# Two layers written out, norms by token tile and half row, turned rows in eight banks, last products by tile

## The chip, the core and the metric

The program runs on one core of one Trainium2 chip. The metric is the device time of one execution, in microseconds (us), as the median of several runs. Engines: TensorE (PE), VectorE (DVE), ScalarE (ACT), GpSimd (POOL) and SyncE (SP), which here issues nearly all DMAs. Each runs its own instruction queue in order, and they wait for one another by semaphores.

## The reference

Two models stand one behind the other. The first is a block of two layers over 256 tokens of width 1024; each layer has a mixer of four branches and a convolved FFN, and each of these ends in an RMS norm whose result is added to x.

```python
for l in range(DEPTH):                     # DEPTH = 2
    h = rms_norm(x, norm_mix_pre[l])
    proj = h @ w_in[l]
    ...
    mix = jnp.concatenate([y_conf, y_sb, y_ret, y_sc], axis=-1) @ w_out[l]
    x = x + rms_norm(mix, norm_mix_post[l])
    f = conv_ffn(rms_norm(x, norm_ffn_pre[l]), ffn_up[l], ffn_conv_w[l], ffn_down[l])
    x = x + rms_norm(f, norm_ffn_post[l])
```

The second block takes that x with a second sequence ctx of 256 tokens and conditioning rows (silu(c) @ ada_w): recurrent memory and attention branches, then a mixture of 32 experts. All is float32.

## The kernel before, in words

Tokens lie on the partitions in two tiles of 128 (t = 0, 1), so x is 128 x 2 x 1024. For a projection x is normalised into xhat, TensorE transposes xhat into PSUM, and ScalarE writes the rows times the gain as a rounded "high" part (high_rows, line 912), VectorE what the rounding lost as a "low" part (low_rows, 1246). Weights are split in the same way in units of 128x1024: ScalarE line 923 the high part, VectorE line 1268 the low part, three units in buffers; each product is made in three passes (high x high, high x low, low x high), so an "up" unit is 24 products of 256 columns.

The two layers are one loop on every engine (loop_layers, lines 760 to 762): the instructions stand once, and waits are on values computed from the loop's register. In a layer, TensorE runs transposes "T" (banks 0 to 3), 24 units of w_in, the branches, the mixer's output M (banks 4 to 7, bank i for token tile i // 2 and column half i % 2; tokens_down, slots 6 and 7), transposes "F" (banks 0 to 3), and 66 units of the FFN, of which 22 "down" units add into D (banks 4 to 7).

The norm after the mixer and the FFN: rms_of_banks squares a tile of 1024 columns out of two banks (line 884, then the root, 885), add_normed takes the reciprocal (1207), multiplies both halves out of PSUM by root and gain (1232) and adds to x (1222). After the mixer rms_of_x then squares the new x per tile, normalise_tile scales it (1213), and transposed turns both tiles (1889); the rows go through high_rows and low_rows in eight pieces of 128x256, and TensorE starts the first unit once all eight are done. After the FFN the same stands at the head of the next pass of the loop. keep_clock is a filler: products of a constant 128x384 (line 1869, psum<-const) whose result nobody reads.

The semaphores x_tile_ready and x_ready count the sums for tile 0 and 1. SyncE loads weights in half slots of 1 MB into a ring of five places; a place is free when its units are split, or, for the mixer's output, after tokens_down (slot_free). GpSimd loads the second block's small tensors, ctx and two rows of ada_b (lines 841 to 850). In the second block, ScalarE works in this order: SiLU of c (1015), squares of x, squares of ctx, evacuation of the "ada" rows (904); TensorE makes ada(0), ada(1), then waits for those rows before each further step, turns x and ctx, and starts products (701 us). The experts' weights (line 824 on) are loaded when slots come free.

Of the kernel before, what the change touches and what calls it, by code (L numbers as in the profile page):

```python
# [13 lines left out]
P = 128  # L14
# [20 lines left out]
ACT_STEPS = 9  # L35
DVE_STEPS = 128
# [96 lines left out]
LAYER_BANKS = [("T", i, i) for i in range(4)]  # L133
# [8 lines left out]
LAYER_BANKS += [("F", i, i) for i in range(4)]  # L142
# [171 lines left out]
def build_program(nc, w, out):  # L314

    with ExitStack() as ctx:
# [222 lines left out]
        x_ready = sem("x_ready")  # L539
# [220 lines left out]
        def loop_layers(eng, layer):  # L760
            with eng.Fori(0, DEPTH) as l:
                layer(l)

        @block.sync
        def _(sp):
# [25 lines left out]
            for l in range(DEPTH):  # L791
                for n in range(len(LAYER_SLOTS)):
# [7 lines left out]
                    if n == 13 and l + 1 < DEPTH:  # L800

                        sp.wait_ge(x_ready, 2 * l + 2)
                        load_mixer_columns(sp, l + 1)
                        load_mixer_rows(sp, l + 1)
                    if n == RING and l:

                        sp.wait_ge(x_ready, 2 * l + 1)
# [27 lines left out]
        def _(pool):  # L835
# [5 lines left out]
            pool.wait_ge(x_ready, 2 * DEPTH)  # L841
# [26 lines left out]
        def _(act):  # L868
            n_step = [0]

            def step(ins, l):
# [3 lines left out]
                act.wait_ge(act_step, l * ACT_STEPS + n_step[0])  # L875
# [12 lines left out]
            def rms_of_x(l, n):  # L888

                rms_of([x[:, t, :] for t in range(TT)], l, lambda t: act.wait_ge(x_ready if t else x_tile_ready, n))  # L890
# [6 lines left out]
            def rms_of_banks(l, key):  # L897

                load_root_table()
                rms_of([psum[:, 4 + 2 * t:6 + 2 * t, :].rearrange("p b n -> p (b n)") for t in range(TT)], l,  # L900
                       lambda t: [take(act, (key, 2 * t + i), l) for i in (0, 1)])
# [4 lines left out]
            def high_rows(key, l, n, col):  # L906

                for i in range(4):
                    b = take(act, (key, i), l)
                    for c in (0, 1):  # L910
                        k = 2 * i + c
                        ins = nc.scalar.activation(hT_split[:, 0, k, :], b[:, c * T:(c + 1) * T], ACT.Copy,
                                                   scale=cols[:, col + k:col + k + 1])
                    ins.then_inc(hT_high_ready, 1)

            def layer(l):
                n_step[0] = 0
                def split(n):
                    if n >= UNIT_BUFFERS:
                        after_unit(act, n - UNIT_BUFFERS, l)  # L920
                    raw, h = unit_weights(n, None)
# [3 lines left out]
                split_until = units_ahead(split, UNITS)  # L925
                rms_of_x(l, 2 * l + 1)
                split_until(UNIT_BUFFERS - 1)
# [23 lines left out]
                act.wait_ge(act_step, l * ACT_STEPS + n_step[0])  # L951
# [26 lines left out]
                split_until(MIX_UNITS + UNIT_BUFFERS - 1)  # L978
# [1645 lines left out]
```

## Time and profile before

| what | us |
|---|---|
| median of 3 runs | 2182.85 |
| lowest and highest | 2179.92, 2186.36 |
| the profiled execution | 2183.95 |
| its span, first to last instruction | 2182.2 |
| TensorE busy in it | 2061.6 |
| VectorE busy | 867.3 |
| ScalarE busy | 595.2 |
| mean granted clock of TensorE | 0.981 of full |

The first block takes the first 665 us, the second block without its experts some 570, and the rest is the experts, in which the DMA engines are nearly always busy. Busy times are averages over stages with different limits: what a norm costs is read from the timeline around it, as the time from TensorE's last product to its next. Filler products count as busy.

### The profile page before, as it was taken

The numbers are of one execution on the slowest core, as the hardware profiler recorded it, in microseconds if no ns is written. First come the engines' busy times: TensorE is split into PE (matmuls) and PEld (weight loads), VectorE is DVE, ScalarE is ACT, GpSimd is POOL, SyncE is SP. The second block draws the span as 40 slices with busy tenths as digits, with TensorE's granted clock in tenths as the row PEclk, the third lists the DMA queues.
The fourth block names the chain that finished last, engine by engine and source line by source line (L and its number), as shares of the span: only waits on it lengthen the run. The fifth ranks groups of instructions, "written<-read, shape, count | busy, mean of one in ns | idle before, by whom it ended". The sixth has DMA issues, their size and how long they took to land.

```text
span 2182.2 us, 27676 instructions
## 1 busy us (share of the span) xinstructions
PE 2061.6 (94%) x11094; PEld 1323.7 (61%) x11094; DVE 867.3 (40%) x1510; ACT 595.2 (27%) x962; POOL 11.6 (1%) x23
## 2 busy tenths in 40 slices
PE   8999999999998998899989999999999999999998
PEld 7869998959995776677789533333333333333332
DVE  6847676947675226553622311111111111111111
ACT  4545555445555323342431100000000000000001
POOL 0000000010000000000000000000000000000000
PEclk9999999999998999999999999999999999999999
DMA  7335553355546534021234699999999999999996
GB/s 293 114 135 200 182 174 141 140 171 192 185 163 231 240 148 162 30 78 52 84 116 154 261 413 413 432 432 432 432 431 431 429 431 432 432 432 432 432 432 291
DMA packets 43237, 589.71 MB, mean 270 GB/s; under 512 B 5185, under 2 KB 5873, under 8 KB 9825
## 3 DMA queue, kind: packets, MB, share of 16 engines
q1 hardware_dynamic: 41392, 583.09, 65.5%
q0 software_dynamic: 1456, 5.01, 0.8%
q8 instruction: 67, 1.10, 0.2%
q10 hardware_dynamic: 288, 0.24, 0.0%
q14 instruction: 34, 0.27, 0.0%
HBM read 587.27 MB, written 1.05 MB: 270 GB/s over the span
## 4 chain that ended last, share of the span: by engine, by line
PE 78%; DMA 13%; DVE 4%; issue 2%; ACT 2%; DVEq 0%; SPq 0%; ACTq 0%
PE psum L1869 46%; PE psum L2299 22%; DMA slots<-exp_w_dram 12%; PE psum L2244 3%; PE psum L2336 3%; PE psum L2411 3%; DVE split_weights L1443 1%; DMA slots<-w_in_dram 0%; DMA slots<-ffn_up_dram 0%; DVE work L1569 0%; PE psum L1889 0%; PE psum L2177 0%; DVE work L1586 0%; DVE split_rows L1246 0%; ACT work L1079 0%
## 5 line engine op out<-in xcount | busy, mean ns | idle before, releaser
L2299 PE MATMUL psum<-slots,work 128*64 128x512 f32 x3072 | 687.2, 601 | 47.8 <-DMA slots<-exp_w_dram 46.3
L2299 PEld LDWEIGHTS psum<-slots,work 128*64 128x64 f32 x3072 | 219.9, 138 | 479.8 <-issue 467.1
L1869 PE MATMUL psum<-split_rows,split_weights 128*128 128x256 f32 (+1 forms) x3744 | 489.8, 293 | 13.0 <-DVE split_rows L1495 4.1
L1869 PEld LDWEIGHTS psum<-split_rows,split_weights 128*128 128x128 f32 x3744 | 473.0, 193 | 33.3 <-issue 12.3
L1268 DVE TENSOR_TENSOR split_weights<-slots,split_weights 128x1024 fp32r<-128x1024 f32 x180 | 219.6, 1224 | 161.3 <-ACT split_weights L923 160.6
L923 ACT ACTIVATE split_weights<-slots 128x1024 fp32r<-128x1024 f32 x180 | 189.9, 1058 | 216.7 <-PE psum L1869 179.1
L1869 PE MATMUL psum<-split_weights,split_rows 128*128 128x512 f32 x1008 | 232.3, 390 | 1.0 <-DVE split_weights L1443 1.0
L1869 PEld LDWEIGHTS psum<-split_weights,split_rows 128*128 128x128 f32 x1008 | 188.3, 188 | 42.5 <-issue 2.5
L1831 DVE TENSOR_SCALAR work<-psum 128x512 f32<-128x512 f32 x32 | 22.0, 689 | 401.4 <-PE psum L2299 401.4
L1869 PE MATMUL psum<-work 128*128 128x128 f32 (+9 forms) x964 | 152.7, 335 | 19.9 <-DVE work L1605 7.1
L1869 PEld LDWEIGHTS psum<-work 128*128 128x128 f32 (+2 forms) x964 | 124.3, 196 | 50.4 <-issue 36.9
L1169 ACT ACTIVATE work<-work 128x512 f32<-128x512 f32 x32 | 20.2, 631 | 478.1 <-DVE work L1831 478.1
L1162 ACT ACTIVATE work<-psum,small 128x128 f32<-128x128 f32 x64 | 24.1, 457 | 352.3 <-PE psum L1869 352.3
L1443 DVE TENSOR_TENSOR split_weights<-slots,split_weights 128x1024 fp32r<-128x1024 f32 x64 | 76.5, 1222 | 106.2 <-ACT split_weights L1020 106.0
L904 ACT ACTIVATE work<-psum 128x512 f32<-128x512 f32 (+3 forms) x150 | 76.1, 523 | 156.2 <-PE psum L1869 119.8
L1020 ACT ACTIVATE split_weights<-slots 128x1024 fp32r<-128x1024 f32 x64 | 66.8, 1055 | 108.6 <-DMA slots<-w_in_dram 62.5
L1844 DVE TENSOR_TENSOR work<-psum,work 128x512 f32<-128x512 f32 x32 | 22.2, 692 | 167.3 <-PE psum L2299 167.3
L1869 PE MATMUL psum<-slots,work 128*128 128x512 f32 x192 | 83.6, 593 | 0.0
L1869 PE MATMUL psum<-const 128*128 128x384 f32 (+2 forms) x208 | 73.0, 496 | 11.2 <-DVEq L1861 6.8
L1412 DVE SCALAR_TENSOR_TENSOR work<-psum,work 128x254 f32<-128x254 f32 (+1 forms) x176 | 76.6, 477 | 1.6
L1869 PEld LDWEIGHTS psum<-const 128*128 128x128 f32 (+1 forms) x208 | 39.9, 199 | 39.5 <-issue 14.3
L2244 PE MATMUL psum<-work 128*128 128x512 f32 (+1 forms) x136 | 63.0, 605 | 0.0
(249 smaller groups left out, 1333.3 us busy)
## 6 DMA issues: line engine op xcount, KB each, us to landing
slots<-exp_w_dram SPq DMA_DIRECT2D x95, 4096.0 KB, 19.0
slots<-w_in_dram SPq DMA_DIRECT2D x56, 1024.0 KB, 6.1
slots<-ffn_up_dram SPq DMA_DIRECT2D x44, 1024.0 KB, 4.8
slots<-ada_w_dram SPq DMA_DIRECT2D x24, 1024.0 KB, 7.0
slots<-ffn_down_dram SPq DMA_DIRECT2D x20, 1024.0 KB, 4.9
slots<-w_out_dram SPq DMA_DIRECT2D x12, 1024.0 KB, 5.0
slots<-w_branch_a_dram SPq DMA_DIRECT2D x4, 1024.0 KB, 8.1
slots<-w_branch_b_dram SPq DMA_DIRECT2D x4, 1024.0 KB, 5.0
```

Of the source, the lines that this page charges most:

```text
L904: nc.scalar.activation(out_, in_, func, **kw).then_inc(evacuated[bank_of(key)], 1)
L923: nc.scalar.activation(unit_weights(n, 0), raw, ACT.Copy).then_inc(w_high_ready, 1)
L1020: nc.scalar.activation(unit_weights2(n, 0), unit_weights2(n, None), ACT.Copy).then_inc(w_high_ready, 1)
L1162: ins = nc.scalar.activation(xgT[:, k, :], b[:, k * P:(k + 1) * P], ACT.Identity, scale=scale2[:, k:k + 1], bias=modT[:, 2 * KC + k, 0:1])
L1268: nc.vector.tensor_tensor(unit_weights(n, 1), unit_weights(n, None)[0], unit_weights(n, 0), ALU.subtract).then_inc(w_split, 1)
L1412: ins = nc.vector.scalar_tensor_tensor(out=o, in0=b[:, c * T:(c + 1) * T - k], scalar=cols[:, at:at + 1], in1=o, op0=ALU.mult, op1=ALU.add)
L1443: nc.vector.tensor_tensor(unit_weights2(n, 1), unit_weights2(n, None), unit_weights2(n, 0), ALU.subtract).then_inc(w_split, 1)
L1869: return nc.tensor.matmul(out_, lhsT, rhs, start=first, stop=last)
L2244: return nc.tensor.matmul(psum[:, i, :], lhsT, rhs, start=first, stop=True, skip_group_check=True)
L2299: return nc.tensor.matmul(b[rows, :], lhs[:, rows], rhs, start=first, stop=last, skip_group_check=True)
L2336: nc.tensor.matmul(psum[:, bank_of((key, n)), :], pick_e, b1_rows[:, c0:c0 + 512], start=False, stop=False, skip_group_check=True)
L2411: ins = nc.tensor.matmul(b[:, c * T:(c + 1) * T], hT_split[:, v, 4 * j + k, c * P:(c + 1) * P], wu[a][:, k, :], start=j + c + k + q == 0, ...
```

## The change

1. The loop is gone: each_layer writes the two layers out, and waits are on constants.
2. After mixer and FFN each norm works on half rows of 512: ScalarE squares a bank (half_square), VectorE multiplies it by the gain at once (times_gain) and, when the root is there, multiplies by its reciprocal and adds to x in one instruction (add_to_x). The squares of the new x are taken by halves too. The FFN's end makes the next norm's squares and xhat itself, for the second block too; the second block no longer does.
3. xhat is turned into eight banks, one for each pair of columns and token tile (turn). high_rows and low_rows work in 16 pieces of 128x128 in the order TILE_ORDER, and the first unit waits pair by pair.
4. The mixer's last products run by token tile; the last two down units are multiplied bank by bank.
5. Fillers move: none before the transposes of tile 0 after the mixer, five behind them; five before "T" of the second layer once bank 4 is added; none at the start behind the transposes and none ahead of the second block.
6. Only two units instead of three are split ahead of the mixer's norm, and one of the next layer's ahead of the FFN's norm.
7. Waits on x_ready become waits on evacuations: the loads of mixer parameters on ("M", 3), of FFN parameters on ("D", 3) of the layer before, GpSimd's loads on ("D", 3) of the last layer.

```diff
+TILE_ORDER = ((0, 0), (1, 0), (0, 1), (1, 1), (2, 0), (2, 1), (3, 0), (3, 1))
...
-LAYER_BANKS = [("T", i, i) for i in range(4)]
+LAYER_BANKS = [("T", i, i) for i in range(8)]
...
-        def loop_layers(eng, layer):
-            with eng.Fori(0, DEPTH) as l:
+        def each_layer(layer):
+            for l in range(DEPTH):
                 layer(l)
...
-            pool.wait_ge(x_ready, 2 * DEPTH)
+            after_evacuation(pool, ("D", 3), DEPTH - 1)
...
+            def half_square(rows, t, half, l):
+                i = 2 * t + half
+                n_squared[0] += 1
+                nc.scalar.activation(flat(soft)[:, 0:512], rows, ACT.Square, accum_out=half_sumsq[:, i:i + 1]
+                                     ).then_inc(half_squared, 1)
+                act.wait_ge(half_squared, n_squared[0])
+                if half == 0:
+                    nc.scalar.activation(half_mean[:, t:t + 1], half_sumsq[:, i:i + 1], ACT.Identity, bias=EPS, scale=1.0 / D)
...
-                split_until(MIX_UNITS + UNIT_BUFFERS - 1)
-                rms_of_banks(l, "M")
-                rms_of_x(l, 2 * l + 2)
+                split_until(MIX_UNITS + 1)
+                load_root_table()
+                for t in range(TT):
+                    for square in (square_of_bank, square_of_sum):
+                        square("M", l, t, 0)
+                        square("M", l, t, 1)
+                        root(t)
...
-                rms_of_banks(l, "D")
+                if l + 1 < DEPTH:
+                    splits[l + 1](0)
+                load_root_table()
+                square_of_bank("D", l, 0, 0)
+                square_of_bank("D", l, 0, 1)
+                root(0)
+                square_of_bank("D", l, 1, 0)
+                square_of_sum("D", l, 0, 0)
+                square_of_bank("D", l, 1, 1)
+                root(1)
+                square_of_sum("D", l, 0, 1)
+                root(0)
+                square_of_sum("D", l, 1, 0)
+                square_of_sum("D", l, 1, 1)
+                root(1)
...
+            def add_to_x(l, n, key, t):
+                inverse_rms(n, t)
+                for half in (0, 1):
+                    cut = slice(512 * half, 512 * half + 512)
+                    nc.vector.scalar_tensor_tensor(out=x[:, t, cut], in0=xhat[:, t, cut], scalar=rinv[:, t:t + 1],
+                                                   in1=x[:, t, cut], op0=ALU.mult, op1=ALU.add
+                                                   ).then_inc(evacuated[bank_of((key, 2 * t + half))], 1)
...
-                tokens_down("M", l, 6, catT, (0, 1), False, False, slot_free)
-                after_evacuation(pe, ("RT", 0), l)
-                tokens_down("M", l, 7, catT, (4, 5), False, True, None)
-
-                keep_clock(("F", 0), l, 6)
-                pe.wait_ge(x_tile_ready, 2 * l + 2)
-                keep_clock(("F", 0), l, 3)
-                transposed("F", l, 2, idle=(("D", 0), 5))
+                for t in range(TT):
+                    tokens_down("M", l, 6, catT, (0, 1), False, False, slot_free if t else None, (2 * t, 2 * t + 1))
+                    after_evacuation(pe, ("RT", 0), l)
+                    tokens_down("M", l, 7, catT, (4, 5), False, True, None, (2 * t, 2 * t + 1))
+
+                pe.wait_ge(xhat_tile_ready, 2 * l + 2)
+                turn("F", l, 0)
+                keep_clock(("F", 4), l, 5)
+                pe.wait_ge(xhat_ready, 2 * l + 2)
+                turn("F", l, 1)
```

TensorE's queue from the mixer's last products to the first up unit, before; const rows of 128x384 are fillers:

```order
L1869 MATMUL psum<-slots,work 128x512 [waits half_slot0_loaded,half_slot4_loaded,bank3_evacuated]
L1869 MATMUL psum<-slots,work 128x512 x7
...
L1869 MATMUL psum<-const 128x384 [waits bank0_evacuated]
L1869 MATMUL psum<-const 128x384 x5
...
L1869 MATMUL psum<-const 128x384 [waits bank0_evacuated,x_tile_ready]
...
L1889 MATMUL psum<-const,work 128x128 [waits bank0_evacuated,xhat_tile_ready]
...
L1889 MATMUL psum<-const,work 128x128 [waits xhat_ready]
...
L1869 MATMUL psum<-const 128x384 [waits bank4_evacuated]
...
L1869 MATMUL psum<-split_rows,split_weights 128x256 [waits bank0_evacuated,weights_split]
```

The same place in the changed kernel, from the transposes on:

```order
L1944 MATMUL psum<-const,work 128x128 [waits bank0_evacuated,xhat_tile_ready]
...
L1911 MATMUL psum<-const 128x384 [waits bank4_evacuated]
L1911 MATMUL psum<-const 128x384 x4
L1944 MATMUL psum<-const,work 128x128 [waits bank4_evacuated,xhat_ready]
...
L1911 MATMUL psum<-split_rows,split_weights 128x256 [waits bank0_evacuated,bank4_evacuated,weights_split]
L1911 MATMUL psum<-split_rows,split_weights 128x256 x5
L1911 MATMUL psum<-split_rows,split_weights 128x256 [waits bank5_evacuated,bank1_evacuated]
...
L1911 MATMUL psum<-split_rows,split_weights 128x256 [waits bank6_evacuated,bank2_evacuated]
...
L1911 MATMUL psum<-split_rows,split_weights 128x256 [waits bank7_evacuated,bank3_evacuated]
```

The fillers ahead of tile 0's transposes are gone, five stand between the tiles, and the first unit's products wait in four steps.

GpSimd's queue ahead of the second block, before:

```order
L847 DMA work<-gate_w_dram 128x128 [waits x_ready]
L847 DMA work<-const_dram 128x1120
...
L847 DMA work<-router_b_dram 128x32
L848 DMA work<-ctx_dram 128x2x1024
L850 DMA work<-ada_b_dram 128x1024 x2
```

And changed:

```order
L846 DMA work<-gate_w_dram 128x128 [waits bank7_evacuated]
L846 DMA work<-const_dram 128x1120
...
L846 DMA work<-router_b_dram 128x32
L847 DMA work<-ctx_dram 128x2x1024
L849 DMA work<-ada_b_dram 128x1024 x2
```

The order is the same; the first wait moved from the second mixer's sum (x_ready 4) to bank 7 of the last FFN.

## Rows read from the trace of the kernel before

**Rows 1.** Page part 4: the chain that ended last, by engine.

```profile
PE 78%; DMA 13%; DVE 4%; issue 2%; ACT 2%; DVEq 0%; SPq 0%; ACTq 0%
```

**Rows 2.** Timeline, first mixer end: start us, us, engine, line, operation, [idle before, releaser].

```profile
116.95 13.90 PE L1869 MATMUL psum<-slots,work 128*128 128x512 f32 x32
...
128.95 1.06 ACT L923 ACTIVATE split_weights<-slots 128x1024 fp32r<-128x1024 f32 x1 [9.31 <-DMA slots<-ffn_up_dram]
...
131.43 1.01 ACT L884 ACTIVATE work<-psum 128x1024 f32<-128x1024 f32 x1
...
133.00 1.41 DVE L1232 SCALAR_TENSOR_TENSOR work<-psum,stats,work 128x512 f32<-128x512 f32 x2
...
141.64 3.03 ACT L912 ACTIVATE split_rows<-psum,work 128x256 fp32r<-128x256 f32 x8 [1.77 <-PE psum L1889]
...
142.58 3.23 DVE L1246 SCALAR_TENSOR_TENSOR split_rows<-psum,work,split_rows 128x256 fp32r<-128x256 f32 x8 [1.73 <-ACT split_rows L912]
...
146.45 18.80 PE L1869 MATMUL psum<-split_rows,split_weights 128*128 128x256 f32 x153
```

**Rows 3.** Timeline, first FFN end and the loop's jump.

```profile
333.40 5.97 PE L1869 MATMUL psum<-const 128*128 128x384 f32 x18
...
337.66 1.28 ACT L884 ACT_TABLE_LOAD   x1 [2.65 <-issue]
...
350.71 7.45 PE L1869 MATMUL psum<-split_rows,split_weights 128*128 128x256 f32 x60 [0.70 <-issue]
```

**Rows 4.** Timeline, from the last FFN to the second block.

```profile
665.00 4.03 PE L1869 MATMUL psum<-const 128*128 128x384 f32 x12
...
673.49 1.06 ACT L884 ACTIVATE work<-work 128x1024 f32<-128x1024 f32 x1 [1.15 <-DVE work L1213]
...
676.05 1.07 ACT L904 ACTIVATE work<-psum 128x512 f32<-128x512 f32 x2
...
701.36 13.02 PE L1869 MATMUL psum<-split_rows,split_weights 128*128 128x256 f32 x96 [4.07 <-DVE split_rows L1495]
```

**Rows 5.** Timeline, the kernel's last norm: squares of half rows on ScalarE.

```profile
2174.04 0.58 ACT L1179 ACTIVATE work<-psum 128x512 f32<-128x512 f32 x1
...
2174.85 0.58 ACT L1179 ACTIVATE work<-psum 128x512 f32<-128x512 f32 x1
...
2175.55 0.29 ACT L1182 ACTIVATE stats<-stats 128x1 f32<-128x1 f32 x1
```

**Rows 6.** Groups by line: 128x128 pieces; busy and mean ns, then idle.

```profile
L1162 ACT ACTIVATE work<-psum,small 128x128 f32<-128x128 f32 x64 | 24.1, 457 | 352.3 <-PE psum L1869 352.3
...
L1698 DVE SCALAR_TENSOR_TENSOR work<-work,small 128x128 f32<-128x128 f32 x16 | 4.3, 352 | 0.0
```

**Rows 7.** Timeline, the start of the first layer.

```profile
10.77 2.18 PE L1889 MATMUL psum<-const,work 128*128 128x128 f32 x16
...
15.02 3.22 DVE L1246 SCALAR_TENSOR_TENSOR split_rows<-psum,work,split_rows 128x256 fp32r<-128x256 f32 x8
...
18.43 11.77 PE L1869 MATMUL psum<-split_rows,split_weights 128*128 128x256 f32 x96 [1.61 <-DVE split_rows L1246]
```

**Rows 8.** Stretches: busy us (instructions) of each engine, then PEclk, DMA share, GB/s.

```profile
342.00:344.00 2.00, 1.34 (x7) 1.34 (x7) 1.64 (x4) 1.97 (x5) 0.00 (x0) 0.60 0.00 0
...
702.00:704.00 2.00, 2.00 (x11) 2.00 (x11) 1.60 (x3) 0.33 (x2) 0.00 (x0) 0.50 0.00 0
```

**Rows 9.** Timeline of GpSimd: its loads for the second block.

```profile
471.05 0.68 POOL L847 DMA_DIRECT2D work<-gate_w_dram  x1 [469.87 <-DVE x_row L1222]
...
474.86 0.71 POOL L848 DMA_DIRECT2D work<-ctx_dram  x1
```

**Rows 10.** DMA issues: xcount, KB each, median us to landing; then GpSimd's loads.

```profile
work<-ctx_dram POOLq DMA_DIRECT2D x1, 1024.0 KB, 9.6
...
small<-cT_dram SPq DMA_DIRECT2D x1, 8.0 KB, 19.4
...
DMA to landing us min/median/max: 2.2/4.6/10.8
```

More of the change, by code:

```diff
@@ L141 @@
 LAYER_BANKS += [("CM", 0, 1), ("CV", 0, 2), ("RT", 0, 3)]
-LAYER_BANKS += [("F", i, i) for i in range(4)]
+LAYER_BANKS += [("F", i, i) for i in range(8)]
 LAYER_BANKS += [("U", g, (2 * (g // 2)) % 4 + g % 2) for g in range(6)]
@@ L886, in rms_of, with rms_of_x @@
                                          ).then_inc(rms_ready, 1)
-            def rms_of_x(l, n):
-                rms_of([x[:, t, :] for t in range(TT)], l, lambda t: act.wait_ge(x_ready if t else x_tile_ready, n))
+            def rms_of_x(l, loaded):
+                rms_of([x[:, t, :] for t in range(TT)], l, loaded)
             def load_root_table():
@@ L923, in split, with layer @@
                     nc.scalar.activation(unit_weights(n, 0), raw, ACT.Copy).then_inc(w_high_ready, 1)
-                split_until = units_ahead(split, UNITS)
-                rms_of_x(l, 2 * l + 1)
-                split_until(UNIT_BUFFERS - 1)
+                return units_ahead(split, UNITS)
+            splits = [layer_splits(l) for l in range(DEPTH)]
+            def layer(l):
+                split_until = splits[l]
+                if l == 0:
+                    act.wait_ge(x_loaded, 16)
+                    rms_of_x(l, lambda t: None)
+                    split_until(UNIT_BUFFERS - 1)
                 act.wait_ge(mix_cols_loaded, 16 * l + 16)
@@ L1269, in split, with layer @@
                                             ).then_inc(w_split, 1)
-                split_until = units_ahead(split, UNITS)
-                normalise(l, 0, 2 * l + 1)
-                split_until(UNIT_BUFFERS - 1)
+                return units_ahead(split, UNITS)
+            splits = [layer_splits(l) for l in range(DEPTH)]
+            def layer(l):
+                split_until = splits[l]
+                if l == 0:
+                    for t in range(TT):
+                        normalise_tile(t + 1, t)
+                    split_until(UNIT_BUFFERS - 1)
                 dve.wait_ge(mix_cols_loaded, 16 * l + 16)
@@ L1860, in _ @@
             dve.wait_ge(x_loaded, 16)
-            dve.sem_inc(x_tile_ready, 1)
-            dve.sem_inc(x_ready, 1)
-            loop_layers(dve, layer)
+            each_layer(layer)
             second()
@@ L1878, in keep_clock, with transposed @@
                     mm(b[:, 0:SPARE], ident, const[:, 0:SPARE])
-            def transposed(key0, l, n, rows=xhat, wait=True, idle=None):
+            def transposed(key0, l, n, rows=xhat, wait=True):
                 for t in range(TT):
@@ L1914, in diagonal_scores, with tokens_down @@
                     done(mm(bs[m][:, T:DIAG], keysT[rows[m], c, P:T], queries[rows[m], c, P:T]), (key, 2 * c + m))
-            def tokens_down(key, l, n, lhs, ks, first, last, free):
+            def tokens_down(key, l, n, lhs, ks, first, last, free, banks=range(4)):
                 wt = slot_ready(pe, n, l, 4)
-                for i in range(4):
+                for i in banks:
                     t, half = divmod(i, 2)
@@ L2528, in _ @@
             pe.wait_ge(zeros_ready, 3)
-            loop_layers(pe, layer)
+            each_layer(layer)
             second()
```

187 lines of the change are left out of this document (102 added, 85 removed).

## Prediction

> **What bounds the kernel now.** First the chain that ended last by line [rows 1]: 78% of it is TensorE, and 22 + 12 points of it are the experts (line 2299 and the DMA of their weights), which the change doesn't touch. Those loads go out when slots come free, so what the part before them wins or loses moves the end by the same amount. I therefore look for the places in the first 700 us at which TensorE has no product to make. There are five, each a norm: the start, the end of mixer and FFN in two layers, and the hand-over to the second block.
>
> At the end of the first mixer [rows 2] the last product's row is 116.95 + 13.90 = 130.85, and the next product starts at 146.45: 15.6 us. Between them stand in a row: squares on ScalarE, which start only at 131.43 because ScalarE first splits a third unit whose half slot is late (128.95, "9.31 idle <-DMA"); sixteen transposes; eight high parts 141.64 to 144.67; eight low parts 142.58 to 145.81. At the first FFN's end [rows 3] it is 333.40 to 350.71, 17.3 us, and ScalarE loads a table at 337.66 after 2.65 us "issue", which is the loop's jump. The loop's second pass has the same rows at its mixer end. At the hand-over [rows 4] products of rows start 701.36 - 665.00 = 36.4 us after the last FFN product.
>
> **The change, part by part.** All times below are on the clock of this trace; its span is 2182.2, its execution 2183.95, and the median of the runs 2182.85, so 1.1 less.
>
> *Mixer end.* The last products now run by tile, so banks M0 and M1 are whole after 6 and 8 of 16 products. One product is 13.90/16 = 0.87: M0 at 122.2, M1 at 123.9, M2 at 129.1, M3 at 130.85. ScalarE splits two units instead of three and is free by 121.2. A half's square with its mean is 0.81 from issue to issue, and its root starts 0.70 after the square [rows 5]. Two multiply-adds of 512 take 1.41 on VectorE [rows 2], and I take half of it, 0.70, for the new multiply of 512 as well; 0.2 for a reciprocal, 0.8 for a normalised tile. Tile 0: squares 122.35 and 124.05, root 124.75, multiply-adds 125.7 to 127.1, squares of the sum, root 128.0, normalised 129.3, all under tile 1's products; transposes follow the last product at 131.0. Five keep-clock products of 0.67 hold TensorE until 135.4. Tile 1: squares 129.25 and 131.0, root 131.7, multiply-adds 132.6 to 134.0, squares of the sum 133.4 and 134.2, root 134.9, normalised 136.25, transposed from 136.35. Now the turned rows, by tile in 16 pieces of 128x128 on each engine. VectorE's is 0.26 (sixteen of line 1698 in 4.3, less 0.35 for the last, by 15) [rows 6]. For ScalarE no row has this form: the 256-column piece is (3.03 less some 0.48 for the last one's own length)/7 = 0.364 [rows 2], the row of a 512 square (0.58) lies 0.43 under that of a 1024 square (1.01 [rows 2]), so 128 columns less are 0.11 less, 0.26; line 1162, 128x128 but with one more operand, comes in fours: 24.1/16 = 1.506, less 0.457, by 3 = 0.35 [rows 6]. I take 0.26, from the row that differs in size alone, and keep 0.35 as the upper bound. Piece (0, tile 1) can start at 136.8; six tiles of two pieces end at 139.9, VectorE at 140.5, and the last 6 of the unit's 24 products (0.123 each) end at 141.3. Before, that unit ended at 146.45 + 2.95 = 149.4. **Gain 8.1**, with 0.35 instead of 0.26 7.0. The third unit's split follows the high parts (139.9 to 142.2) and is wanted at 144.2: hidden. Its load waits for slot_free, now 3.5 us later (127.4), and lands near 132: hidden too.
>
> The ScalarE page of the Trainium skill ("ScalarE: Activation LUTs", What ACT_TABLE_LOAD costs) prices such a piece at 186 + 107 + 93 - 93 = 293 ns, by which the gain would be some 0.3 smaller; no run here shows that form.
>
> *First FFN end.* The last two units are multiplied by bank: 24 products in 5.5 us make D0 at 329.2, D1 330.6, D2 332.0, D3 333.35. ScalarE first splits the next layer's unit 0 (328.0 to 329.1), then table, squares 330.4 and 331.2, root 331.9; VectorE adds tile 0 at 332.8 to 334.2 and tile 1 at 336.0 to 337.35; roots of the sum at 336.05 and 338.2; normalised 338.2 and 339.55; transposes 338.3 and 339.65. High parts end at 343.2, low 343.85, unit 0 at 344.65; unit 1, whose split now stands behind the high parts, runs 345.6 to 348.5. Before, unit 1 ended at 350.71 + 5.9 = 356.6. **Gain 8.0.** The loop's jump and two table loads go with it. The convolution taps wait on constants now, but line 1297 already runs at VectorE's pace, so the unrolling brings nothing there.
>
> *Start.* Low parts from 15.02 [rows 7]: the first pair of tiles at 16.6, all at 19.2, unit 0 ends at 20.0 instead of 21.4: 1.4. But TensorE's six keep-clock products of 4 us are gone, and it idles from 12.95.
>
> *The clock.* After the keep-clock products end at 339.4 [rows 3] TensorE idles, and in 342 to 344 the granted clock is 0.60, partly 1.2 GHz [rows 8]; it comes back before the products. At the hand-over the products after 701.36 themselves run at 0.50, 1.2 GHz. In the changed kernel the fillers before the mixer's transposes are gone and products start into whatever clock is left. A slow stretch costs 0 to 1.7 us (the slow stretch around 703 held some 3.4 us, of which half is lost). I charge 0.8 at each layer's norm and 1.1 at the start: start +0.3, mixers 2 x 7.3, FFN 7.2. Sum of gains 22.1.
>
> *Hand-over.* Here the change takes time. GpSimd's loads for the second block waited for the second mixer (x_ready 4: issued from 471.05 [rows 9], 200 us before use). They now wait for bank D3's evacuation in the last layer. By the steps above that is 668.5. Queued behind this wait are six small loads, 3.81 us of issue, then the 1 MB of ctx, then the two rows of ada_b. ctx lands 9.6 us after issue [rows 10]: 668.65 + 3.81 + 9.6 = 682.1. ScalarE squares it (before at 673.49), and behind those squares on ScalarE stand the evacuations of the ada rows (676.05 [rows 4]), for which TensorE waits before the next ada product. 2.56 us as before plus 1.28 for a table that the SiLU, now after the roots, evicts: 685.9 instead of 676.05, 9.9 late. SyncE's ada loads, which before found no other queue, share the engines then; ctx by equal sharing lands some 2 us later still. **Loss 12.** Below: the median landing of GpSimd's loads, 4.6, would make it 4.9 for ctx. Above: an 8 KB load issued in the full queue of the start landed after 19.4 [rows 10], which would make it 19.7.
>
> The DMA page of the Trainium skill ("DMA: Bandwidth & Descriptors", Anatomy of one DMA - SWDGE (gpsimd) path) fits 2.0 us + bytes/436e3 for such a load, 4.4 for ctx. By it the loss would be near 5, which is the first rival below; the row's 9.6 has other transfers in flight, and here there are more.
>
> **Sum:** 2183.95 - 22.1 + 12 = 2173.9, so 2174.
>
> **The rivals.**
> *The late loads cost little.* For it: most of the small loads land sooner than ctx, and TensorE idles here anyway while ScalarE works off the norms. Against it: in the trace ctx took 9.6 us without SyncE's loads beside it. With a loss of 5: 2183.95 - 22.1 + 5 = 2166.9.
> *The gain per norm is half.* The clock is low at every boundary and 128-column pieces take 0.35: 8.1 - 1.1 - 1.7 = 5.3 each, 15.9 with the start at -0.5 15.4; loss 14: 2182.5, no measurable change.
> *The late loads cost more than all norms give, the slower case.* One mechanism: the software queue's loads, ctx and ada_b, share with SyncE's 1 MB halves, and VectorE waits for both ada_b rows before it scales ctx. With gains of 22.1 the kernel is slower from a landing of 9.6 + 12.2 = 21.8 us on, and measurably from 28; the 19.4 of the start is near. With 30 us: 2192.
> *The change doesn't do what it says:* half rows bring no overlap because banks still come whole at the end. The order of products speaks against it: M0 is whole 8.6 us before M3. Included in the second case.
>
> **How the numbers follow.** About 0.3% (6.5 us) is what a measurement can tell from no change. Forecast 0.60 (its own range 2169 to 2178.5), little loss 0.13, half gain 0.22, slower 0.05. Net gains over 6.5 us are the first two and a little of the third: faster 0.74, same 0.21, slower 0.05. The range leaves out the far ends: the best sum, 25.7 - 8 = 17.7, is 2166, and the half-gain case 2182.5: 2166.5 to 2182.5.
>
> **What would show it.** In the changed trace: the gap from the last mixer product to the end of the first up unit near 10.5 us instead of 18.5, twice; from the last FFN product of layer 0 to the end of the second unit near 15 instead of 23; GpSimd's first load near 647 (668.65 less the 22 won before it) instead of at a mixer's end, behind VectorE's add; ctx's squares waiting for a DMA; 128x128 ScalarE pieces at 0.25 to 0.35. It is wrong if GpSimd's loads start at the mixer's end, if ctx's squares don't wait for them, or if the granted clock stands at half for more than 3 us at a norm.

## The result

| | before | changed |
|---|---|---|
| median of 4 runs, us | 2183.07 | 2165.62 |
| lowest and highest | 2179.92, 2186.36 | 2163.21, 2167.73 |
| the profiled execution's span | 2182.2 | 2164.5 |

The changed kernel is 17.45 us faster, ratio 0.992, 95% interval 0.9901 to 0.9938 (13.5 to 21.6 us). Timed once more in five rounds it was 2165.37 against 2179.89: ratio 0.9929, 0.9914 to 0.9944 (12.2 to 18.7 us). The forecast was 2174.0, 9 us under the median and 10 under the profiled execution, and the range ended at 2166.5: the direction was right and the size too small, by 8.4 us.

**The profile after.** Page part 4, the chain by engine, answers to [rows 1]:

```profile
PE 79%; DMA 13%; DVE 5%; ACT 2%; issue 1%; POOL 0%; SPq 0%; DVEq 0%; ACTq 0%
```

Timeline of the changed kernel, first mixer end (start us, us, engine, line, operation, [idle before, releaser]), against [rows 2]:

```profile
117.54 13.90 PE L1911 MATMUL psum<-slots,work 128*128 128x512 f32 x32
...
122.89 0.60 ACT L900 ACTIVATE work<-psum 128x512 f32<-128x512 f32 x1 [1.15 <-PE psum L1911]
...
129.04 0.75 DVE L1251 TENSOR_SCALAR work<-x_row,stats 128x1024 f32<-128x1024 f32 x1
129.76 0.60 ACT L900 ACTIVATE work<-psum 128x512 f32<-128x512 f32 x1 [0.95 <-PE psum L1911]
...
135.91 0.75 DVE L1251 TENSOR_SCALAR work<-x_row,stats 128x1024 f32<-128x1024 f32 x1
...
137.19 3.21 ACT L929 ACTIVATE split_rows<-psum,work 128x128 fp32r<-128x128 f32 x12 [0.49 <-PE psum L1944]
...
138.61 7.62 PE L1911 MATMUL psum<-split_rows,split_weights 128*128 128x256 f32 x58 [0.80 <-DVE split_rows L1279]
```

The mixer's products end at 131.44. Tile 0's first square starts at 122.89, 8.6 us ahead of that, and its rows are normalised by 129.8. The first product of the FFN starts 7.2 us after the mixer's last one; before it was 15.6.

The first FFN's end, against [rows 3]:

```profile
326.14 3.49 PE L1911 MATMUL psum<-const 128*128 128x384 f32 x10 [0.20 <-DVE x_row L1267]
330.81 1.09 PE L1944 MATMUL psum<-const,work 128*128 128x128 f32 x8 [1.18 <-DVE work L1251]
332.20 1.09 PE L1944 MATMUL psum<-const,work 128*128 128x128 f32 x8 [0.30 <-DVE work L1251]
334.09 3.53 PE L1911 MATMUL psum<-split_rows,split_weights 128*128 128x256 f32 x24 [0.80 <-DVE split_rows L1279]
338.15 4.10 PE L1911 MATMUL psum<-split_rows,split_weights 128*128 128x256 f32 x32 [0.52 <-DVE split_weights L1300]
```

The hand-over, against [rows 4] and [rows 9]:

```profile
645.89 0.68 POOL L846 DMA_DIRECT2D work<-gate_w_dram  x1 [644.71 <-DVE x_row L1267]
...
648.45 6.17 PE L1911 MATMUL psum<-slots,small 128*32 128x512 f32 x32 [6.26 <-ACT small L1055]
...
652.15 2.87 SPq L787 DMA_DIRECT2D slots<-ada_w_dram  x3
...
658.79 1.06 ACT L883 ACTIVATE work<-work 128x1024 f32<-128x1024 f32 x1 [10.40 <-DMA work<-ctx_dram]
...
662.64 1.07 ACT L921 ACTIVATE work<-psum 128x512 f32<-128x512 f32 x2
663.32 1.84 PE L1911 MATMUL psum<-work 128*128 128x2 f32 x8 [8.70 <-issue]
```

GpSimd's loads start at 645.89, ctx's squares wait 10.40 us for a DMA, and the evacuation of the ada rows (662.64) stands behind them. The first product that uses such a row starts at 663.32, 21.1 us after the first block's end. The second block's first product from split rows starts at 688.15.

**Where the time went**, by stage, from TensorE's timelines of five executions. "The third slot's end" is the end of the products made from the first three weight slots of a layer; "hand-over" is the time from the last FFN product to the second block's first product from split rows. Stage ends are modelled ends of products, so they can differ by 0.2 from a row's.

| stage, us | before | before again | changed | again | again |
|---|---|---|---|---|---|
| start to the third slot's end | 41.6 | 41.9 | 42.2 | 42.3 | 41.2 |
| last mixer product to first down product, layer 0 | 50.4 | 50.3 | 42.2 | 42.2 | 42.2 |
| last down product to the third slot's end, layer 1 | 40.3 | 40.1 | 32.5 | 32.5 | 32.5 |
| last mixer product to first down product, layer 1 | 49.8 | 49.7 | 42.2 | 42.2 | 43.3 |
| **first block ends at** | 665.2 | 665.2 | 642.2 | 642.3 | 642.3 |
| hand-over, to the second block's first product | 36.2 | 32.9 | 46.0 | 46.6 | 43.9 |
| from there to its output projection | 420.9 | 420.6 | 418.0 | 420.8 | 418.3 |
| projection to the experts | 122.5 | 122.5 | 122.5 | 122.5 | 122.5 |
| the experts to the end | 937.5 | 938.7 | 935.8 | 936.6 | 936.7 |
| **span** | 2182.2 | 2179.8 | 2164.5 | 2168.7 | 2163.8 |

Between the two profiled executions: first block -23.0, hand-over +9.8, second block -2.8, experts -1.7, sum -17.7. The rest of both layers (89.3 of mixer, 152.27 of FFN, each twice) is the same to 0.02.

### The profile page after: what moved, and what is told of

Same layout as the page of the kernel before. It is cut to its first block, busy times and chain, and to the rows that moved or that the text cites. A ratio compares the mean times of both kernels' runs of the same rounds, so it can differ in the third digit from the quotient of the medians.

```text
span 2164.5 us, 26772 instructions
## 1 busy us (share of the span) xinstructions
PE 2036.1 (94%) x11014; PEld 1308.4 (60%) x11014; DVE 872.0 (40%) x1550; ACT 605.8 (28%) x1040; POOL 11.4 (1%) x23
## 4 chain that ended last, share of the span: by engine, by line
PE 79%; DMA 13%; DVE 5%; ACT 2%; issue 1%; POOL 0%; SPq 0%; DVEq 0%; ACTq 0%
PE psum L1911 47%; PE psum L2348 22%; DMA slots<-exp_w_dram 12%; PE psum L2293 3%; PE psum L2385 3%; PE psum L2463 3%; DVE split_weights L1488 1%; ACT work L900 0%; DVE work L1613 0%; DVE work L1336 0%; DMA work<-router_b_dram 0%; PE psum L2226 0%; DVE work L1630 0%; ACT work L1118 0%; DMA x_row<-x_dram 0%
## 5 line engine op out<-in xcount | busy, mean ns | idle before, releaser
L1208 ACT ACTIVATE work<-work 128x512 f32<-128x512 f32 x32 | 20.2, 631 | 478.2 <-DVE work L1875 478.2
L1911 PEld LDWEIGHTS psum<-slots,work 128*128 128x128 f32 x192 | 36.2, 190 | 42.8 <-issue 42.6
L2385 PE MATMUL psum<-work 128*128 128x512 f32 x128 | 59.2, 604 | 0.0
```

The lines of the kernel that those rows point to most:

```text
L1911: return nc.tensor.matmul(out_, lhsT, rhs, start=first, stop=last)
L2385: nc.tensor.matmul(psum[:, bank_of((key, n)), :], pick_e, b1_rows[:, c0:c0 + 512], start=False, stop=False, skip_group_check=True)
```

## The experiments

Besides the forecast's account (gains at the norms, a loss by late loads) stood these rivals: that the loads cost little; that the order on ScalarE makes the loss; that writing the layers out is what helps; that pieces or halves alone do. Where a single time is given there is one execution, and what is read from it is its trace.

**Early loads** (e1). The changed kernel with

```diff
-            after_evacuation(pool, ("D", 3), DEPTH - 1)
+            after_evacuation(pool, ("M", 3), DEPTH - 1)
```

> The changed kernel, but GpSimd's loads for the second block wait for bank M3's evacuation in the last layer (the mixer's end, as before) and not for D3's. Theory (the late loads cost the hand-over): ScalarE's squares of ctx no longer wait 10.40 us for a DMA; the ada rows go out right behind the first ada products, which end at 648.45 + 6.17 = 654.6, so TensorE's next row product starts near 655.2 instead of 663.32: 8 us less, 2157.5. Rival (the loads cost little, the table load and the SiLU behind the norm make the loss): ctx is there, but the rows go out no earlier than 660: at most 3 us less, 2162.5 or more.

Measured: 2158.15 (2155.56 to 2160.83), ratio to before 0.9897, 0.9868 to 0.9925; hand-over 35.8. That is 7 us under the changed kernel's medians, and 8 to 11 in the hand-over. Its timeline:

```profile
647.42 6.14 PE L1911 MATMUL psum<-slots,small 128*32 128x512 f32 x32 [6.26 <-ACT small L1055]
...
653.49 1.05 PE L1911 MATMUL psum<-work 128*128 128x2 f32 x8
```

The row product comes 12.3 us after the first block's end instead of 21.1. The late loads are the loss, as forecast. Issued at 453.59, behind five of SyncE's 1 MB loads (from 443.27 on), ctx takes longer to land here, but nothing waits for it:

```profile
work<-ctx_dram POOLq DMA_DIRECT2D x1, 1024.0 KB, 14.7
```

**Late loads alone** (e2), in the kernel before:

```diff
-            pool.wait_ge(x_ready, 2 * DEPTH)
+            pool.wait_ge(x_ready, 2 * DEPTH + 1)
```

> The kernel before, but GpSimd's loads wait for the last FFN's sum (x_ready 5). Theory: first load at 670.9, ctx lands 3.81 + 9.2 to 9.6 later, at 684.1, so its squares start 10.6 later than at 673.49 and the end with them: 2183 + 10.6 = 2193.7. Rival (loads share the engines with nothing and land in the median 4.6): ctx at 679.3, 5.8 later: 2189. Rival (the loss is a matter of the changed kernel's order on ScalarE, not of the loads): within 3 of 2183.

Measured: 2205.41, ratio 1.011 (1.0082 to 1.0138), hand-over 55.9: a loss of 20 to 23 there and 24 in the medians, twice the expected. **Missed.** The issue groups show why; ctx's row in e2, in the changed kernel and in e7 below (KB each, us to landing):

```profile
work<-ctx_dram POOLq DMA_DIRECT2D x1, 1024.0 KB, 16.9
```
```profile
work<-ctx_dram POOLq DMA_DIRECT2D x1, 1024.0 KB, 9.2
```
```profile
work<-ctx_dram POOLq DMA_DIRECT2D x1, 1024.0 KB, 15.0
```

And in e2's timeline SyncE's loads go out with GpSimd's (ctx's at 673.69); the squares wait for VectorE, which waits for ada_b:

```profile
670.10 2.04 SPq L788 DMA_DIRECT2D slots<-ada_w_dram  x3
...
670.38 0.67 POOL L847 DMA_DIRECT2D work<-gate_w_dram  x1 [669.20 <-DVE x_row L1222]
...
693.06 0.16 DVE L1207 RECIPROCAL stats<-stats 128x1 f32<-128x1 f32 x1 [5.67 <-DMA work<-ada_b_dram]
...
694.97 1.06 ACT L884 ACTIVATE work<-work 128x1024 f32<-128x1024 f32 x1 [23.47 <-DVE work L1213]
```

So two things add up there. One is a collision of the two queues: ctx takes 7.7 us longer than in the changed kernel and lands near 690.6. The other is xhat's normalising, which in the kernel before stands on VectorE behind its wait for ada_b and in the changed kernel ahead of it: ctx's squares start 4.4 us after ctx's landing. The second is read from this trace and was not tested by itself.

**SiLU first** (e7). Does the changed kernel escape that collision by chance of its order? In it SyncE's loads go out at 652.15, since the ada products wait for the SiLU, which now follows the norm. The edit takes the SiLU of c ahead of the last norm:

```diff
                 if l + 1 < DEPTH:
                     splits[l + 1](0)
+                else:
...
+                    nc.scalar.activation(siluc[:, :, 0:2], cT, ACT.Silu).then_inc(siluc_ready, 1)
                 load_root_table()
...
-                nc.scalar.activation(siluc[:, :, 0:2], cT, ACT.Silu).then_inc(siluc_ready, 1)
```

> The changed kernel with the SiLU of c ahead of the last norm's table load. The ada products then run right behind the last FFN product (642.2 to 645.9), and SyncE's next loads go out near 644 to 648 instead of from 652.15, together with GpSimd's from 645.89. Theory (the two queues' loads share the engines, as when the late loads alone were put into the kernel before: ctx landed after 16.9 instead of 9.2): ctx lands 15 to 17 us after issue, the hand-over is 51 to 54 instead of 46.5. Rival (loads don't hinder each other here): the table load of 1.28 us behind the norm goes, hand-over 45.

Measured: hand-over 50.1, ctx landed after 15.0, 2175.09. Its timeline:

```profile
644.36 2.04 SPq L787 DMA_DIRECT2D slots<-ada_w_dram  x3
646.15 0.68 POOL L846 DMA_DIRECT2D work<-gate_w_dram  x1 [644.97 <-DVE x_row L1268]
...
664.86 1.06 ACT L883 ACTIVATE work<-work 128x1024 f32<-128x1024 f32 x1 [17.74 <-DMA work<-ctx_dram]
```

The hand-over is 3.5 to 6.1 us longer than in the three executions of the changed kernel: an earlier SiLU makes the kernel slower, the collision is real, and the late SiLU spares ctx from it. The size is 1 us under what was expected.

**Written out only** (e3): the kernel before with a Python loop over the layers instead of the register loop.

> The kernel before with its two layers written out and nothing else changed. Theory: only the loop's jump goes, 1.4 us at the first FFN's end (2.65 us of issue on ScalarE, of which some is hidden), and the second block is as before: 2181.5. Rival (written-out layers are what made the second block of the changed kernel 4.5 us shorter than before's): 2178 or less, with the gain behind 700 us.

Measured: 2180.52 against 2181.5, ratio 1.0002 (0.9986 to 1.0017). The first FFN's end is 39.7 instead of 40.1 to 40.3, second block 420.7, experts 937.7. The jump is worth 0.4 to 0.6, not 1.4, and what the changed kernel wins behind 688 is not from this. The rival that writing out is what helps is refuted.

**Last products by bank** (e5):

```diff
-                for t in range(TT):
-                    tokens_down("M", l, 6, catT, (0, 1), False, False, slot_free if t else None, (2 * t, 2 * t + 1))
-                    after_evacuation(pe, ("RT", 0), l)
-                    tokens_down("M", l, 7, catT, (4, 5), False, True, None, (2 * t, 2 * t + 1))
+                tokens_down("M", l, 6, catT, (0, 1), False, False, slot_free)
+                after_evacuation(pe, ("RT", 0), l)
+                tokens_down("M", l, 7, catT, (4, 5), False, True, None)
```

> The changed kernel with the mixer's last products in the old order, weight slot by weight slot over all four banks. Bank M0 is then whole after 10 of 16 products instead of 6, M1 after 12 instead of 8, 3.5 us later; M2 and M3 as now. Theory (tile 0's norm hides under tile 1's products, and that is worth something): ScalarE reaches tile 1's root 1.5 us later, so the stretch from the last mixer product to the first down product is 42.2 + 1.5 = 43.7, twice, and the kernel 3 us slower. Rival (the half rows and the 128x128 pieces carry it all): 42.2 to 42.5. Rival (tile 0's norm stands whole behind the products): 45.7 or more.

Measured: 43.76 and 43.75 where the changed kernel has 42.22 (the one execution took 2168.72): 1.5 each, as worked out. The order by tile is worth a fifth of a mixer norm's gain.

**Rows in four banks** (e6): LAYER_BANKS with four T and F, `turn` into halves of them, `high_rows` and `low_rows` in 128x256.

> The changed kernel with xhat turned into four banks and high_rows and low_rows in eight pieces of 128x256, the first unit still waiting pair by pair. The pieces then start only when tile 1 is turned, but eight of 0.36 take 2.9 us where twelve of 0.26 are left. Theory (the 128x128 pieces bring little): from the last mixer product to the first down product 42.5 to 42.8 instead of 42.22, in both layers, and 32.7 to 33.0 instead of 32.46 at the first FFN's end. Rival (tile 0's pieces done ahead are worth their whole length, 4 x 0.26 and the low ones behind): 43.3 or more. Rival (fewer, longer instructions are better): 42.0 or less.

Measured: 42.52, 32.40 and, with the clock low under the first unit (0.50 in 454 to 456), 43.78; the execution took 2162.36. The FFN's end came out under the 32.7 to 33.0 expected: **missed there.** The eight banks and 128x128 pieces bring 0.3 at the mixer and nothing at the FFN's end. What is left of a mixer norm's gain, some 6 of 8 us, must lie in the rest of the change at this place: the half rows, the two units split ahead instead of three, the fillers that left and the first unit's waits in steps. These were not taken apart, so which of them carries it is not shown.

**No fillers** (e8): both keep_clock calls of five out of the changed kernel.

> The changed kernel without the five fillers between the turned tiles and without those at the second layer's head. The prediction charged 0.8 us for a low clock at each of three norms, and the clock stayed at 1.00. Theory (the fillers held it): without them the granted clock falls to half ahead of the first unit, and each of the three stretches is 0.8 to 2.5 us longer, 2.4 to 7.5 in all. Rival (the gaps are short enough by themselves): clock 1.00 still, 42.2, 32.5 and 42.2 us as now.

Measured: 43.28, 33.03 and 43.09, so 1.1, 0.6 and 0.9 longer, 2.5 us in all (2173.29 for the one execution). Stretches of it (busy us of PE, PEld, DVE, ACT, POOL, then PEclk, the granted clock as a share of 2.4 GHz, DMA share, GB/s):

```profile
136.00:138.00 2.00, 1.16 (x6) 1.16 (x7) 1.79 (x5) 1.26 (x6) 0.00 (x0) 0.50 0.98 414
138.00:140.00 2.00, 1.83 (x9) 1.46 (x8) 1.77 (x7) 2.00 (x9) 0.00 (x0) 0.50 1.04 438
```

The changed kernel in the same place:

```profile
136.00:138.00 2.00, 1.09 (x8) 0.86 (x8) 1.84 (x6) 1.51 (x7) 0.00 (x0) 1.00 1.02 430
138.00:140.00 2.00, 1.39 (x12) 1.42 (x12) 2.00 (x9) 2.00 (x10) 0.00 (x0) 1.00 1.01 426
```

The fillers hold the 2.4 GHz level there; without them TensorE is idle for 4.4 us ahead of the second tile's transposes, and these and the first products run at 1.2. With them it fell in some executions all the same (43.3 in the last column of the table): at 3 of 18 mixer ends in the nine executions that have these fillers and the changed kernel's norms.

**Fillers at the start** (e4): five between the turns of the seventh and the eighth bank.

```diff
                 for i in range(4):
+                    if idle and i == 3:
+                        keep_clock((key, 4 * t + i), l, idle)
...
-                turn("T", l, 1)
+                turn("T", l, 1, 0 if l else 5)
```

> The changed kernel with five filler products of 128x384 at the start, between the turned rows' seventh and eighth bank. Theory (the cold clock made the start a loss of 0.6 where 1.4 was there to be had): the clock is 1.00 when the products start at 16.6, and the first unit's stretch ends 2.0 us earlier: 2163.6. Rival (the eighth bank, turned at 16.3, holds the first unit up, or low_rows does): 0.5 us less or none, 2165 to 2166.

Measured: from the first transpose to the third slot's end 29.8 us, against 31.5, 31.5 and 30.7 in the changed kernel and 30.8 before. The changed kernel at the start, and e4:

```profile
18.00:20.00 2.00, 2.00 (x12) 2.00 (x11) 1.04 (x5) 0.00 (x0) 0.00 (x0) 0.50 0.91 382
```
```profile
18.00:20.00 2.00, 1.91 (x16) 1.67 (x15) 1.29 (x6) 0.00 (x0) 0.00 (x0) 1.00 0.89 374
```

The stage wins 0.9 to 1.7 us, somewhat under the 2.0 worked out; the whole kernel was 2167.34 (2164.88 to 2168.31), where its first block's end, 1.8 us earlier, can't be seen. **The total did not show it.**

**Each kernel again** (c1 before, c2 and c3 changed), for what differs from execution to execution.

> The kernel before once more, for its trace. From the second block's first product to the first product of its output projection (701.36 to 1122.23) it took 420.9 us, with the layers only written out 420.7, with late loads only 421.0; in the changed kernel and its two variants so far 418.0, 418.0, 417.7. Theory (this 2.9 us belongs to the changed kernel and is no chance of one execution): 420.5 to 421.2 again. Rival (chance): some value down to 418. The experts to the end: anything from 936 to 939 by either, their loads' landing differs by that from run to run.

> The changed kernel once more, for its trace. Theory: the same stretch 417.6 to 418.3 again; hand-over from the last FFN product to the second block's first product 46.0 as before, the first block's end within 1 us of 642.2 by where x lands. Rival (chance): a stretch nearer 421, or a hand-over more than 1.5 us off.

> The changed kernel timed again in five rounds, to bound how much of the 17.45 us is the change. By the stages that repeat in all traces (end of the first block 22.9 us earlier, the hand-over 46.5 against 33.0 in two executions of before and 36.2 in the profiled one) the change is worth 9.4 to 12.6 us; the second block's stretch (418 or 421) and the experts (934 to 939) differ from execution to execution. Theory (they differ by chance alone): a ratio of 0.9942 to 0.9957, 9 to 13 us. Rival (the changed kernel falls into the short forms more often): a ratio near 0.992 again, 15 to 18 us.

Measured: the table's columns. The hand-over of before was 32.9 this time, and 33.0 in e3; the 36.2 of the profile shown ahead is the long form. Timelines of the two executions, the same sixteen products:

```profile
683.71 3.61 PE L1869 MATMUL psum<-slots,small 128*32 128x512 f32 x16
```
```profile
682.15 1.92 PE L1869 MATMUL psum<-slots,small 128*32 128x512 f32 x16
```

The kernel before gave 420.6, as expected. But the stretch of 418 was 420.8 in c2: the expectation that it belongs to the changed kernel fell as stated. And c3's ratio, 0.9929, lies between theory and rival, nearer to the rival; its interval, 0.9914 to 0.9944, leaves room for both. Two parts of the difference in the second block are a wait for a split unit and fourteen rows of fillers, in the profiled execution of before and of the changed kernel:

```profile
821.92 16.66 PE L1869 MATMUL psum<-split_weights,split_rows 128*128 128x512 f32 x72 [0.99 <-DVE split_weights L1443]
...
856.04 5.57 PE L1869 MATMUL psum<-const 128*128 128x384 f32 x14
```
```profile
841.55 4.67 PE L1911 MATMUL psum<-const 128*128 128x384 f32 x14
```

The wait for a split unit goes back to DMA: the split itself waits for its weight slot. The seven loads issued around it land after this long (KB each, median us), before and changed:

```profile
slots<-w_in_dram SPq DMA_DIRECT2D x7, 1024.0 KB, 9.0
```
```profile
slots<-w_in_dram SPq DMA_DIRECT2D x7, 1024.0 KB, 8.0
```

That repeats. In all four executions of the kernel before and its variants the same loads take 8.9 to 9.0 and TensorE waits 0.8 to 1.7 us; in eleven of the twelve of the changed kernel and its variants they take 7.6 to 8.4 and it waits 0.3 or not at all. The exception is e8, with 9.5 and a wait of 0.7. Why the loads land sooner is not shown.

**Shifted in time** (p1, p2): more fillers ahead of the very first transposes. A filler is two rows, so the transposes came 19.7 and 38.6 us later instead of 10.1 and 20.2. Of this 4.9 us did not reach what follows, since the start's norm now ran under the fillers: the work behind was shifted by 14.8 and 33.6. The test is the same.

> The changed kernel with 30 more fillers ahead of the very first transposes: the work of TensorE is shifted by 10.1 us and is else the same. The last expert's sixteen products took 5.3 us at a low clock in every execution that came to them at 2145.7 or later (2145.7 to 2174.1, five) and 3.65 at full clock in every one that came at 2145.5 or sooner (nine). Here they start near 2149. Theory (where such a low stretch falls hangs on the moment, counted from the start, and not on what was changed): 5.3, and the experts from their first product to the end 937.5 to 938.7. Rival (it hangs on the changed kernel's code): 3.65 and 935.8 to 936.8. The second block's stretch tells the same way if it is 420.2 or more, but it was long in some executions of the changed kernel too.

> The same with 60 more fillers, 20.2 us later: the changed kernel then runs at the moments at which the kernel before ran. Theory (the moment decides): the last sixteen products, near 2159, take 5.3; the second block's stretch 420.2 or more, as in all four executions of before; total 2186 or more. Rival (the changed code decides): 3.65, a stretch near 418, total 2184 or less.

Measured: second block 418.4 and 418.6, experts 936.8 and 936.3; spans 2178.5 and 2197.4, which without the shift are 2163.7 and 2163.8. The last expert's first sixteen products in before, in the changed kernel and in p2:

```profile
2154.80 5.35 PE L2299 MATMUL psum<-slots,work 128*64 128x512 f32 x16 [1.92 <-DMA slots<-exp_w_dram]
```
```profile
2138.95 3.65 PE L2348 MATMUL psum<-slots,work 128*64 128x512 f32 x16 [1.92 <-DMA slots<-exp_w_dram]
```
```profile
2171.64 3.65 PE L2348 MATMUL psum<-slots,work 128*64 128x512 f32 x16 [1.92 <-DMA slots<-exp_w_dram]
```

My theory, that the moment decides, is refuted: at 2171.64 they still take 3.65. By count, the second block's stretch was under 418.8 in eight and over 420.1 in four executions of the changed kernel and its variants, over 420.5 in all four of the kernel before and its variants; the last products took 5.3 in one of twelve against four of four. That is more than chance makes likely, but what in the changed code does it stays open. On average over all these executions, twelve and four, the second block's stretch is 1.6 us shorter with the changed code and the experts 2.0 (933.2 to 938.1 against 937.5 to 938.7).

**The best of it** (e10): the edits of e1, e4 and e7 together (early loads, start fillers, SiLU first), and on ScalarE

```diff
+                ada_rows_out(0, 1)
                 act.wait_ge(ctx_loaded, 16)
                 act.wait_ge(xhat_ready, 2 * L2 + 1)
                 rms_of([ctx_row[:, t, :] for t in range(TT)], l, ...
-                ada_rows_out(0, 1, 2, 3)
+                ada_rows_out(2, 3)
```

> The changed kernel with four things: GpSimd's loads at the second mixer's end (8 us in the run with that alone), five fillers at the start (1.5 us from the turned rows to the end of the third weight slot's products), the SiLU ahead of the last norm, and the first two ada rows evacuated ahead of ctx's squares. Theory (the order on ScalarE holds the ada chain, 35.8 us of hand-over with early loads alone): the first row product comes some 7 us sooner, the ada weights' landing then leads, hand-over 29 to 31, kernel 2150 to 2153. Rival (the weights' landing leads at once): hand-over 34 or more, 2156 or more.

Measured: 2151.47 (2150.78 to 2153.63), ratio to before 0.9866, 0.9848 to 0.9884; hand-over 27.7:

```profile
642.30 3.64 PE L1913 MATMUL psum<-slots,small 128*32 128x512 f32 x32
...
646.94 1.07 ACT L921 ACTIVATE work<-psum 128x512 f32<-128x512 f32 x2
...
647.62 1.02 PE L1913 MATMUL psum<-work 128*128 128x2 f32 x8 [1.68 <-issue]
...
670.09 5.27 PE L1913 MATMUL psum<-split_rows,split_weights 128*128 128x256 f32 x23 [4.07 <-DVE split_rows L1541]
```

28 us under the kernel before and 14 under the changed one. The hand-over is 1.3 us shorter than the expected 29 to 31. The ada products start at once (642.30) and the first row product 5.3 us after the first block's end, where e1 with early loads alone has 12.3. So with the loads out of the way, the early SiLU and the early rows together win 8 us of hand-over; how much of it is the SiLU's, which alone made a loss, was not taken apart.

## Why the prediction was wrong in size

*The views and the places* were right: five norms, nothing else changed in the first block.

*Mixer end: right.* Taken relative to the last product, the forecast's steps came out within 0.3 us: squares, root, normalised tile 1 (forecast 136.25, measured 136.66 with products ending 0.6 later), a piece of 128x128 on ScalarE (3.21 - 0.34)/11 = 0.26, where 0.34 is taken for the last piece's own length. Forecast 8.1 without the clock, 7.3 with it; measured 8.2 and 7.5.

*First FFN end: right mechanism, 0.6 low.* 7.2 forecast, 8.0 without the clock; measured 7.8. The second unit did wait for its split, as forecast (338.15, "0.52 <-DVE split_weights").

*The clock: the charge was in the wrong places.* I charged 0.8 us at each norm because fillers ahead of the transposes were gone, but the five between the tiles held 1.00 in the profiled execution; what falls without them is 1.1, 0.6 and 0.9 (e8). At the start, where I charged 1.1, the clock cost more in the profiled execution: products ran from 16.60 at 0.50 up to 22, and the stage lost 0.6 where +0.3 was forecast. In c3 it was shorter than before by 0.4 to 0.7, so the forecast there is neither borne out nor refuted.

*The sum of gains*, 22.1 forecast: 23.0.

*Hand-over: right mechanism, 2.2 too high.* Forecast 12 (9.9 by ctx's landing, 2 by contention); 9.8 between the profiled executions, 11.0 between the short forms of either (43.9 and 32.9). The term that failed is the contention, 2 us by equal sharing: SyncE's loads went out only at 652.15, 2.6 us after ctx, and ctx landed after 9.2. Where they do collide, it is 15.0 and 16.9: the rival "late loads cost more" had a real mechanism, which this order of work keeps out, and equal sharing is too little for it. The rival "little loss" was refuted by e1, although its 2166.9 is the nearest of all the numbers to the result: that is luck, since the loss was 10 to 11 and not 5, and time won elsewhere made up for it.

By the fit of the Trainium skill's page "DMA: Bandwidth & Descriptors" (Anatomy of one DMA - SWDGE (gpsimd) path) ctx would land after an estimated 4.4 us. These traces do not agree: it took 9.2 with SyncE's loads issued 2.6 us behind it, and up to 16.9 with them issued ahead. No run here has the load alone.

*The step that failed most*: "what the part before them wins or loses moves the end by the same amount". It put what happens behind the hand-over at nothing without a reason, and that is 4.5 of the 7.6 us between forecast and span: the changed kernel was 2.8 us shorter in the second block and 1.7 in the experts, in work that the change does not touch. About 1.0 of it is the wait for a weight slot that landed sooner, 0.9 the fillers at a low clock (5.57 us in before, 4.67 after) and 1.7 the last expert's products (5.35 against 3.65); the remaining 0.9 lies in several smaller differences. On average over all executions 3.6 of the 4.5 repeats; its cause stays open. The rest of the 7.6 is 0.9 at the norms and 2.2 at the hand-over. That the medians are 8.4 apart and not 7.6 is rounding and the changed kernel's profiled execution, 0.6 above its median. The second timing, a gain of 14.5 us, would put the miss at some 5.4 us instead of 8.4. The range gave nothing for 1480 us of such work, though the runs shown differed by 6.4 us; with 3 us more to each side it would have held the result.

## What to carry to other kernels

A norm between two stages can be attacked from its producer too: order the last products so that one tile is whole early, and its norm hides under the rest of them. Here that order alone was worth 1.5 of 8.2 us, and the half rows and what came with them the larger part. Ask of every wait that is moved to a later event what its engine then loads beside which other queue, and whether someone waits in order behind the data: here one moved wait took back 7 to 11 us, and one line brought it home. Take a range from more than the changed stages: a stage that nobody touched differed by 2.7 us between two executions of the same kernel (418.0 and 420.8).

## What the runs showed of the hardware

- The same sixteen products of 128x512 took 1.92 us in one execution and 3.61 in another of the same kernel, at granted clocks of 1.00 and 0.50, and a whole hand-over 32.9 or 36.2: how long TensorE stays at the lower level after a wait is not the same each time.
- A 1 MB load on GpSimd's queue landed after 9.2 us with SyncE's 1 MB loads starting 2.6 us behind it, and after 15.0 and 16.9 with these starting 5.4 and 3.6 us ahead of it.
- Five fillers were enough to hold 2.4 GHz over the 7.2 us between two runs of products at 15 of 18 mixer ends, in place of fourteen before; without any, 2.5 us were lost in three places.
